# The recurrence's projections as three split products, with the reads' projection moved into the phase before it

## What is computed

```
h = rms_norm(x);  xx = token_shift(h) - h;  x_j = h + xx * mu[j]      # six blends: r w k v a g
r = x_r @ W_r;  k = x_k @ W_k;  v = x_v @ W_v;  g = x_g @ W_g           # 1024 x 2048 each
decay = f(tanh(x_w @ w1) @ w2);  a = sigmoid(a0 + (x_a @ a1) @ a2)      # low rank, 64
kk = normalised(k * k_k);  k = k * (1 + (a - 1) * k_a)
S_t = S_{t-1} diag(decay_t) - (S_{t-1} kk_t)(a_t kk_t)^T + v_t k_t^T;   y_t = S_t r_t
y = (head_norm(y) + sum(r * k * r_k) * v) * silu(g);   out = y @ W_out
```

## Time and profile before

| | |
|---|---|
| three runs, us | 2399.33, 2401.20, 2402.07 |
| median, us | 2401.2 |
| the profiled execution: its time, us | 2397.99 |
| its span, first to last instruction, us | 2396.2 |
| TensorE busy over the span | 89% |
| VectorE busy over the span | 46% |
| mean granted TensorE clock | 0.952 |

### The profile page before, as it was taken

How to read it: one execution, slowest core, us unless ns; L and a number is a source line. 1 busy time by engine, 2 the same in 40 slices (tenths; PEclk the granted TensorE clock), 3 DMA queues, 4 the chain that set the end, 5 groups by cost and what they waited for, 6 DMA issues and landing times. The chain is left out here.

```text
span 2396.2 us, 45378 instructions
## 1 busy us (share of the span) xinstructions
PE 2122.2 (89%) x18748; PEld 1473.7 (61%) x18748; DVE 1095.6 (46%) x1741; ACT 860.7 (36%) x1339; POOL 182.5 (8%) x201
## 2 busy tenths in 40 slices
PE   5987998988999898779899999898987788999798
PEld 3654555544454455557688888666773366888685
DVE  5614554444445444442544443225525635666421
ACT  3223333433333334331422332225535535454311
POOL 2001111111211111000000000000112100000000
PEclk8999999999999999889999999999987789999899
DMA  3210100100111000031322321314100022323221
GB/s 119 70 64 29 38 30 30 39 30 29 39 33 35 30 30 29 2 123 53 115 89 95 105 96 62 106 35 139 53 1 0 1 70 88 105 88 105 87 87 54
DMA packets 42721, 145.81 MB, mean 61 GB/s; under 512 B 5696, under 2 KB 8000, under 8 KB 42048
## 3 DMA queue, kind: packets, MB, share of 16 engines
q1 hardware_dynamic: 42416, 141.26, 18.1%
q10 hardware_dynamic: 144, 2.10, 0.2%
HBM read 141.24 MB, written 2.10 MB: 60 GB/s over the span
## 5 line engine op out<-in xcount | busy, mean ns | idle before, releaser
L141 PE MATMUL bank<-h_hi,conv_whi 128*128 128x512 f32 x512 | 200.4, 391 | 10.3 <-DVE h_lo L148 10.3
L142 PE MATMUL bank<-h_lo,conv_whi 128*128 128x512 f32 x512 | 200.0, 391 | 0.0
L143 PE MATMUL bank<-h_hi,conv_wlo 128*128 128x512 f32 x512 | 199.9, 390 | 0.0
L772 PE MATMUL bank<-lerp_k,w_k 128*128 128x512 f32 x256 | 140.4, 636 | 14.3 <-ACT ld L644 14.3
L141 PE MATMUL bank<-h_hi,up_whi 128*128 128x512 f32 x352 | 138.2, 393 | 9.9 <-DVE h_lo L148 9.0
L142 PE MATMUL bank<-h_lo,up_whi 128*128 128x512 f32 x352 | 137.9, 392 | 0.0
L143 PE MATMUL bank<-h_hi,up_wlo 128*128 128x512 f32 x352 | 137.8, 392 | 0.0
L772 PE MATMUL bank<-lerp_r,w_r 128*128 128x512 f32 x256 | 134.1, 629 | 0.0
L1247 DVE TENSOR_TENSOR x<-x,bank 128x512 f32 (+1 forms) x32 | 22.0, 688 | 241.9 <-PE bank L143 241.9
L772 PE MATMUL bank<-lerp_v,w_v 128*128 128x512 f32 x256 | 126.1, 617 | 0.0
L141 PE MATMUL bank<-y_hi,out_whi 128*128 128x512 f32 x256 | 103.4, 404 | 23.0 <-DVE y_lo L148 14.4
(11 more groups left out here) (343 smaller groups left out, 4627.8 us busy)
## 6 DMA issues: line engine op xcount, KB each, us to landing
conv_raw<-in_w_conv SPq DMA_DIRECT2D x64, 512.0 KB, 3.4
up_raw<-in_w_up SPq DMA_DIRECT2D x44, 512.0 KB, 3.9
out_raw<-in_w_out SPq DMA_DIRECT2D x32, 512.0 KB, 3.9
down_raw<-in_w_down SPq DMA_DIRECT2D x16, 704.0 KB, 4.1
in_raw<-in_w_in SPq DMA_DIRECT2D x20, 512.0 KB, 3.6
g_raw<-in_w_g SPq DMA_DIRECT2D x16, 512.0 KB, 3.4
w_k<-in_w_k SPq DMA_DIRECT2D x16, 512.0 KB, 3.4
w_r<-in_w_r SPq DMA_DIRECT2D x16, 512.0 KB, 3.4
```

The costliest lines, as they stand in the source:

```text
L141: pe.matmul(out, w_hi[:, w], x_hi[:, k, :], start=(first and n == 0), stop=False)
L142: pe.matmul(out, w_hi[:, w], x_lo[:, k, :], start=False, stop=False)
L143: m = pe.matmul(out, w_lo[:, w], x_hi[:, k, :], start=False, stop=(last and n == len(ks) - 1))
L772: m = pe.matmul(G[(q + k) % 2][:, :], ring[name][:, j * P:(j + 1) * P], lerp[name][:, j, :], start=(j == 0), stop=(j == DC - 1))
```

## The change

- In the recurrence k and v are no longer float32 matmuls but the three products of the split form, 24 for each. Their weights are split while the kernel runs: one ScalarE copy and one VectorE subtraction of 128x1024 for each of k and v in every step but the last two, and four before the first. Blends for k and v are kept as pairs of parts.
- The projection for r leaves the recurrence. It runs in `lerp_phase` as 16 more jobs in split form behind the 16 of the gate, with the blend for r put where that for the gate was; each result is copied by ScalarE and stored to a DRAM tensor `r_all`, and each step of the recurrence loads its tile `rraw` from there. The phase ends when all stores have landed.
- `gemm` hands out single products, so the arguments of `fill` are new: 2; 3, 2, 2, 0, 0 ahead of the levels' `up_products` and 6, 4, 6, 6, 0 behind; 4, 4, 1, and 2 in each round; then the rest. They add up to more than the 48 products that there are.
- ScalarE takes `kk` and `kraw` out of the bank one place earlier, and two tiles share memory with others (`nn` with `ld`, `bon` with `kraw`).

The core of the diff:

```
-                K["lerp"] = {n: sbt(left, f"lerp_{n}", [P, DC, T]) for n in "rkv"}
+                K["lerp"] = {n: pair(left, f"lerp_{n}", DC) for n in "kv"}
+                K["r_all"] = nc.dram_tensor("r_all", (IC, P, T), F32).ap()
...
+
+        SPLIT = [(name, j) for name in "gkvr" for j in range(DC)]
...
+                sp.dma_start(raw[:, n % RING, :], ins["w_g" if n < IC else "w_r"][n % IC])\
+                    .then_inc(S(f"w{n % RING}"), 16)
+
+            def store(c):
+                sp.wait_ge(S("r_out"), c + 1)
+                sp.dma_start(K["r_all"][c], thg[:, c % 2, :]).then_inc(S(f"r_stored{c % 2}"), 16)
+
...
+            for c in range(IC - JOBS, IC):
+                store(c)
+            for k in range(2):
+                sp.wait_ge(S(f"r_stored{k}"), 16 * IC // 2)
 
...
+                        act.wait_ge(S(f"r_stored{c % 2}"), 16 * (c // 2))
...
+        raw = {n: sbt(ctx, f"w_{n}", [P, DC * P]) for n in "kv"}
+        wts = {n: [sbt(ctx, f"w_{n}_{part}", [P, DC * P], F32R) for part in ("hi", "lo")] for n in "kv"}
         lora = sbt(ctx, "w_lora2", [P, P])
...
-                    need(sp, S("gemm"), NJ * (c - 1) + 3 + n)
-                    sp.dma_start(ring[name][:, :], ins["w_" + name][c]).then_inc(S("w_" + name), 16)
-                    if n == 0:
+                for name in "kv":
+                    need(sp, S("wlo_" + name), c)
+                    sp.dma_start(raw[name][:, :], ins["w_" + name][c]).then_inc(S("w_" + name), 16)
+                    if name == "k":
+                        need(sp, S("gemm"), NJ * (c - 1) + 2)
                         sp.dma_start(lora[:, :], ins["lora2"][c]).then_inc(S("w_lora"), 16)
+                need(sp, S("bon"), c)
+                sp.dma_start(rraw[:, :], K["r_all"][c]).then_inc(S("r_in"), 16)
...
+            def split(n, name):
+                act.wait_ge(S("w_" + name), 16 * n + 16)
+                need(act, S("gemm"), NJ * (n - 1) + (3 if name == "k" else 4))
+                act.activation(wts[name][0][:, :], raw[name][:, :], ACT.Copy).then_inc(S("whi_" + name), 1)
...
                 swapped(c, 4)
...
-                    evacuate(c + 1, 1 - q, 0, kraw[:, :], [("kp", c + 1)])
                     key_square(c + 1)
+                if more(c):
+                    split(c + 2, "k")
                 act.wait_ge(S("mv_mm"), c + 1)
...
-                    evacuate(c + 1, 1 - q, 1, rraw[:, :], [("bon", c + 1), ("rt", c + 1)])
-                    evacuate(c + 1, 1 - q, 2, vT[:, :], [("bonus", c + 1), ("turn_mm", 4 * (c + 1))])
+                    evacuate(c + 1, 1 - q, 1, vT[:, :], [("bonus", c + 1), ("turn_mm", 4 * (c + 1))])
+                if more(c):
+                    split(c + 2, "v")
                 act.wait_ge(S("y_mm"), c + 1)
...
+            split(0, "k")
+            split(0, "v")
...
+                for k, name in enumerate("kv"):
+                    hi, lo = wts[name]
                     for j in range(DC):
+                        w = slice(j * P, (j + 1) * P)
                         if j == 0:
-                            pe.wait_ge(S("w_" + name), 16 * (n + 1))
+                            pe.wait_ge(S("wlo_" + name), n + 1)
                             bank_free(n, 2 + k)
-                        m = pe.matmul(G[(q + k) % 2][:, :], ring[name][:, j * P:(j + 1) * P],
-                                      lerp[name][:, j, :], start=(j == 0), stop=(j == DC - 1))
+                        pe.matmul(G[k][:, :], hi[:, w], lerp[name][0][:, j, :], start=(j == 0), stop=False)
+                        yield
+                        pe.matmul(G[k][:, :], hi[:, w], lerp[name][1][:, j, :], start=False, stop=False)
+                        yield
+                        m = pe.matmul(G[k][:, :], lo[:, w], lerp[name][0][:, j, :], start=False, stop=(j == DC - 1))
                         if j == DC - 1:
...
-                        fill(1)
+                    fill((3, 2, 2, 0, 0)[lv])
                     up_products(c, lv)
                     if lv == 1:
                         turn(c, 1)
-                    if lv < 4:
-                        fill(1)
+                    fill((6, 4, 6, 6, 0)[lv])
 
                 pe.wait_ge(S("turned"), 4 * c + 4)
...
+                        fill(2)
                 m.then_inc(S("y_mm"), 1)
-                fill(24)
+                fill(48)
                 if not last:
...
+                dve.wait_ge(S("whi_" + name), n + 1)
+                split_lo(dve, wts[name][1][:, :], raw[name][:, :], wts[name][0][:, :]).then_inc(S("wlo_" + name), 1)
+
             def key_factor(n):
...
                         dve.transpose(both(inv[:, :, :, :]), both(invT[:, :, :, :])).then_inc(S("inv"), 1)
                     else:
                         up.then_inc(S("inv"), 1)
+                if more(c):
...
-
+                if more(c):
+                    split(c + 2, "v")
```

More of the change, by code:

```diff
@@ L302, in lerp_phase @@
     RING, JOBS = 2, 4
+    N = 2 * IC
     with ExitStack() as ctx:
@@ L383, in _ @@
                     act.activation(hidden[LORA:P, :], bank[1][LORA:P, :], ACT.Copy).then_inc(S("hid"), 1)
[L384 to L385 removed]
+                if n < IC:
+                    need(act, S("gate"), n - 1)
+                    act.activation(thg[:, n % 2, :], bank[2 + n % JOBS][:, :], ACT.Tanh, scale=0.5).then_inc(S("thg"), 1)
+                    if n >= JOBS and n < JOBS + DC:
+                        hi(DC + 2 * (n - JOBS))
+                        hi(DC + 2 * (n - JOBS) + 1)
+                else:
+                    c = n - IC
+                    if c < 2:
+                        act.wait_ge(S("gate"), IC)
+                    else:
+                        act.wait_ge(S(f"r_stored{c % 2}"), 16 * (c // 2))
+                    act.activation(thg[:, c % 2, :], bank[2 + n % JOBS][:, :], ACT.Copy).then_inc(S("r_out"), 1)
+                if n == IC - 1:
+                    for e in range(3 * DC + 2, 4 * DC):
+                        hi(e)
         @block.tensor
@@ L401, in job, with pair_by_chunk @@
                 if ks[-1] == DC - 1:
                     m.then_inc(S("g_mm"), 1)
+            def pair_by_chunk(n, first):
+                for k in range(DC):
+                    pe.wait_ge(S("lerp_lo"), first + k + 1)
+                    for s in range(2):
+                        job(n + s, [k])
             def hiddens(n):
                 lo, hi = ((0, LORA), (LORA, P))[n]
+                pe.wait_ge(S("wl"), 16 * n + 16)
                 for j in range(DC):
                     pe.wait_ge(S("lerp"), DC * n + j + 1)
-                    m = pe.matmul(bank[1][lo:hi, :], wl[:, j, lo:hi], tmp[n][:, j, :], start=(j == 0),
+                    m = pe.matmul(bank[1][lo:hi, :], wl[:, j, :], tmp[n][:, j, :], start=(j == 0),
@@ L424, in _ @@
+            for n in range(JOBS, IC):
+                job(n)
+                if n == JOBS + 1:
                     hiddens(1)
-            with pe.Fori(2, IC // JOBS) as i:
-                for s in range(JOBS):
-                    job(i, s)
+            pair_by_chunk(IC, 3 * DC)
+            for n in range(IC + 2, N):
+                job(n)
         @block.vector
@@ L566, in cols, with more @@
             return slice(n * HD, (n + 1) * HD)
+        def more(c):
+            return not (isinstance(c, int) and c >= IC - 2)
         @block.sync
@@ L792, in loras @@
                     bank_free(n, j)
-                    pe.matmul(G[(q + j) % 2][:, :], lora[rows[j], :], hidden[rows[j], :], start=True, stop=True)\
+                    pe.matmul(G[j][:, :], lora[rows[j], :], hidden[rows[j], :], start=True, stop=True)\
                         .then_inc(S("gemm"), 1)
@@ L858, in step @@
                 first = isinstance(c, int) and c == 0
-                more = iter(()) if last else gemm(c + 1, 1 - q)
+                dense = iter(()) if last else gemm(c + 1, 1 - q)
                 def fill(k):
                     for _ in range(k):
-                        next(more, None)
+                        next(dense, None)
                 pe.wait_ge(S("bet"), c + 1)
@@ L1138, in _ @@
             reads(0, 0)
+            split(1, "k")
             bonuses(0, 0)
+            split(1, "v")
             run(step)(dve)
```

208 lines of the change are left out of this document (116 added, 92 removed).

## The result

The changed kernel takes 2429.4 us (median of four runs, 2423.8 to 2430.2) against 2400.3 for the kernel before on the same chip: a ratio of 1.0123, 95% interval 1.0100 to 1.0147. It is slower by 29 us where I forecast 12. The profiled execution spans 2427.3 us, 31.1 more than that of before.

The account below looks back on a forecast made before the run. Dense TensorE products bound the kernel only where no other engine was late. Front +93.2, prologue -8.3, steps -90, stalls -3 gave -8; clock +20 made +12 on 2401.2: 2413 us, range 2388 to 2433.

Parts of the forecast that it names:

- hand-over from gate to r: Front phase: 4.9 us until both jobs of r's first pair can run, 0.7 used: +4.2, bounds 2 and 7.
- phase's end, prologue, gate's jobs: Last store landing before the front phase closes, +2.3; prologue without r and with shorter k and v, -8.3.
- step at full clock, loop's turn apart: Each of 15 recurrence steps sheds 6.0 us, -90 in all; bounds -5.2 and -6.6 a step.
- the turn's waits: "Issue" stalls in the scores, some in every second step, would lie under `LA`'s lateness: -3 over all.
- clock: Longer TensorE gaps, mainly ahead of `NTG`, bring about 1.1 falls a step at 1.2 us: +20, bounds 0 and 40.
- Start of a step: Split ahead of `LA` moves it from 1.23 to 2.40 us, first level from 5.28 to 6.03: +0.9 with the mask.
- Both covers: Mid-step, k's ScalarE copy fits under 1.63 us of idle, VectorE's subtraction under 4.02 ahead of `nn`: 0.
- Rounds: Two products replace one matmul in each round; seven rounds go from 8.6 to 6.0 us, with the start -3.2.
- Rival 4: Rounds not shortened, as VectorE's `kk`, `yc`, `bet` set them; 24 us fail to come: 2420; chance 0.05.
- Tail: Step's end: without five matmuls, 1.25 us from seventh round to `bonus_sums`, -3.4 a step, before +0.3 for contention.
- I take +0.3: Step's end: `rt` and `bon` meet GpSimd's addition on shared SBUF interfaces, costing 0.3 us a step.
- rival 3: Clock falls at every such gap, two a step at 1.2 us, +36 in 15 steps: 2429; chance 0.10.

Follow-up runs that it names:

- Experiment 11: Written-out changed kernel with early reads and v's split ahead of the bonuses, plus r's second weight split before further blends at the hand-over: 2363.3 us, 0.9860.
- experiment 3: Changed kernel with VectorE's split of v's weights put ahead of the bonuses instead of behind: 2426.2 us, 1.0116.
- Experiment 12: Experiment 11's kernel with the split of v's next weights also put ahead of VectorE's gate multiplication: 2358.1 us, 0.9823.
- 5: Changed kernel, still looped, with VectorE's `rt` and `bon` moved from the step's end to behind `decayed_keys`: 2403.4 us, 1.0024.
- experiment 7: Changed kernel with the recurrence's loops written out and the reads (`rt`, `bon`) moved early: 2370.6 us, 0.9895.
- 9: Written-out changed kernel with early reads, plus the split of v's next weights ahead of the bonuses: 2366.4 us, 0.9869.

## Why the prediction was right in its direction and wrong in its size

Against my +12 the profiled execution has +31.1, 19 more. Term by term:

| term | predicted | measured | excess |
|---|---|---|---|
| hand-over from gate to r | +4.2 | 11.4 | +7.2 |
| phase's end, prologue, gate's jobs | -6.0 | -8.3 | -2.3 |
| step at full clock, loop's turn apart | -6.0 x 15 | -5.5 x 15 | +7.5 |
| the turn's waits | -3 | +0.9 to +2.3 | +4 to +5 |
| clock | +20 | about 22 | +2 |

- **Front phase.** The 86.7 us of products are right to a few tenths. *The hand-over is the term that failed*, and above its bound of 7. What I counted, the time until both jobs of the pair can run, was about right: 5.2 us (145.40 to 150.63) for 4.9, and 3.9 of waits (1.53 and 2.35) for 4.2. What I left out came behind it. The pair works chunk by chunk and frees its weights together at its end, so the next job waits once more, 1.81; and I had priced no fall of the clock in this phase, where the half level held for 6.8 and 3.4 us. In seven of ten profiles only 3.4 us of half level followed, and the hand-over costs 8.4, above the bound all the same; so 3 of the 11.4 belong to this execution. Experiment 11 brings the 8.4 to 5.8. Behind it the phase's end was 0.8 us cheaper and the prologue 1.1; the gate's own jobs had ended 0.3 earlier in this execution.
- **Start of a step.** `LA` at 1.99 at full clock instead of 2.40; the first level at 5.6 instead of 6.0. At the half level `LA` comes at 2.04 to 2.06, and there the scores alone would hold it (experiment 3), which I had not seen. The products with `NTG` start 34.1 us behind the step's start in both kernels at full clock, where I had +0.3.
- **Middle.** Both covers held. The bracket at `NTG` is 2.02 to 2.05, forecast 2.1.
- **Rounds.** From `NTG`'s first product to the seventh round 12.09 before, 9.18 now and 9.02 in a step at full clock: -3.1 against -3.2. Rival 4 is excluded.
- **Tail: the size that was wrong in the steps.** From the seventh round to `bonus_sums` I had 1.25 and 0.3 for contention, 1.55; it is 2.08, 2.16 at full clock. VectorE's `rt` takes 1.59 instead of 0.68, 0.9 more, while `bon` keeps its 0.74. The step that failed is "I take +0.3": GpSimd's work of 5.8 us (560.95 to 566.74) keeps its length while the rounds lost 2.6, so its addition now lies wholly under `rt`. The Trainium skill (GPSIMD Engine Reference, section Specifications) has the rule on the shared interfaces that I had set aside in size: the sum that went by it alone, 0.9 a step, was the nearer one, though it put the loss on two operations where the trace has it on one. Experiment 12 shows the same at another place: 1.22 becomes 1.90. As these products stand last in the step, the tail's wait is the dearest place: moving the reads out (5 and 7) took 1.8 us from the step at full clock (46.3 to 44.5).
- **The loop's turn.** I had let the stalls of the kernel before shrink under the later `LA`. *This step failed too: they did not shrink.* Taken from the loops written out, the turn costs 15.2 us before and 16.1 now by the medians (15.0 and 17.3 by the 15 steps of the profiles). The waits marked "issue" went from 10.2 us to 18.5; in the step shown 1.75 for `bon` and 3.21 at the turn are paid one behind the other.
- **Clock.** Written out, the steps take 716.5 us, and 15 x 46.3 = 694.5 at full clock: 22 for the clock and what small stalls remain (25 if the short first step, 43.4 us, is left out). The amount was near my 20, the *place was wrong*. I had put half of the falls behind the gap at `NTG`. Of the 19 falls in the changed kernel's steps 5 come at that gap; 14 lie at the steps' end and start. Seven of these come 0.2 to 0.6 us into the wait of 1.8 for `bon`, which follows the rounds' gaps of 0.36, as from 617.6; two in the wait at the turn, as from 866.8; five around the end of `bonus_sums`. In experiment 12 the gap ahead of `NTG` is in every step, 2.05 us, and 13 steps in a row hold 1.00. So rival 3's mechanism, a fall at every such gap, is refuted for this gap, though its time, 2429, was hit. The Trainium skill (TensorE: Matmul & The Clock Gate, section A second HAM failure mode) describes short idles between groups of matmuls that make the clock go to and fro; the trace agrees for the end of the steps, where several of them stand in a row, and for the single one of 2.05 only in part: 5 falls of the changed kernel come at it, none in the 13 steps of experiment 12.

The direction follows from two large terms, +85 and -73 as forecast, which nearly cancel; +90 and -59 as measured. The largest single loss, 26 of the 29 us, is that the reads stayed at the end of the step. Moving them alone makes the looped kernel about equal to the one before (1.0024), not faster. In the written-out form, where the kernel before stands at 0.9946, the same idea with early reads runs at 0.9895, and at 0.982 with the hand-over and the split moved too: a gain of 13 and of 26 us like for like.

**Open.** Why one gap is followed by the half level in some steps and not in others isn't settled: in experiment 7 six steps fell behind the same 2.0 us at `NTG` behind which no step from 364 us on fell in experiment 12. The 4.2 us between experiments 7 and 9 is within the noise of the two, and no moved operation explains it. Their profiles differ in the falls (10 and 6) and in small waits marked "issue" (4.9 us and none), which two steps at full clock in experiment 7 bore without being longer (44.4 and 44.6). Why TensorE stands at the turn is argued from the written-out forms, not seen in a record of its own.

## What to carry to other kernels

When dense work is taken out from between dependent small work, price the tail of the loop body first: what had been hidden behind the last dense products (here two VectorE operations and 0.9 us of contention) is then paid whole, and moving such operations a few lines up may be worth more than the dense work saved. Before trusting a phase that is lengthened by a second pass over the same buffers, follow the hand-over for two pairs of buffers, not for one. And two large terms of opposite sign need their small companions listed, since these make the result.

## What the runs showed of the hardware

- At a hardware loop's turn TensorE stood 2.4 to 3.3 us with no engine to wait for behind a step's end without dense work, and 2.4 to 3.5 behind nine dense products, there in one piece or two; written out, the same code has no such wait. The loop of six turns cost 15 us in one kernel and 16 in the other, each within about 4.
- VectorE operations on two SBUF tiles took 1.59 to 1.69 instead of 0.68 us (128x512) and 1.90 instead of 1.22 (128x1024) beside one GpSimd addition of 1.26 to 1.27 us.
- Single idle times of 2.02 to 2.05 us of TensorE left the clock at 1.00 in 13 steps in a row (experiment 12); in experiment 7 the same gap was followed by the half level in six steps. Seven times in the changed kernel the clock fell within the 1.8 us that follow a row of gaps of 0.36. In the hand-over it fell at the wait of 2.35 us in all ten profiles, at that of 1.81 in three of them.
- Stores of 256 KB to a DRAM tensor took 4.3 us to land (median of 16, beside weight loads), and loads of the same size from it 2.9, where the output's stores took 2.0 to 2.1.
